# First modulation tile in two halves, third tile ahead of two weight quarters, two weight roundings ahead of the squares

## The reference

```
cond = silu(c)
mod = cond @ mod_w + mod_b                      # 1024 x 6144
shift1, scale1, gate1, shift2, scale2, gate2 = split(mod, 6)
h = rms_norm(x, norm1_g) * (1 + scale1) + shift1
proj = h @ w_in                                 # 1024 x 5832
q_m, k_m, v_m, o_m, i_m, f_m, c_q, c_kv, k_r, gate_pre = split(proj)
...                                             # mLSTM and latent attention, merged
x = x + gate1 * mixer
...                                             # mixture of experts, then the second block
```

## Time and profile before

| what | us |
|---|---|
| runs | 1007.26, 1012.1, 1012.5 (median 1012.1) |
| the profiled execution | 1009.17 |
| its span, first to last instruction | 1007.4 |
| PE, DVE, ACT, POOL busy | 961.9, 492.1, 385.9, 380.5 |

### The profile page before, as it was taken

How to read it: one execution, slowest core, us unless ns; L and a number is a source line. 1 busy time by engine, 2 the same in 40 slices (tenths; PEclk the granted TensorE clock), 3 DMA queues, 4 the chain that set the end, 5 groups by cost and what they waited for, 6 DMA issues and landing times.

```text
span 1007.4 us, 15224 instructions
## 1 busy us (share of the span) xinstructions
PE 961.9 (95%) x6116; PEld 705.8 (70%) x6116; DVE 492.1 (49%) x863; ACT 385.9 (38%) x617; POOL 380.5 (38%) x249
## 2 busy tenths in 40 slices
PE   8999999999999999888898999999999999999997
PEld 4876687777878444443343899777556789999996
DVE  2355177536144632321222513546766378777775
ACT  4343354445343321211121644544552353434342
POOL 3665666435773055353320689730003400000000
PEclk9999999999999999999999999999999999999999
DMA  9997964333769999999999788523224466353511
GB/s 371 403 382 305 356 196 122 105 109 101 250 215 422 377 419 416 408 412 411 412 411 370 282 317 263 146 84 112 98 74 139 164 272 236 140 229 146 220 72 42
DMA packets 50554, 252.08 MB, mean 250 GB/s; under 512 B 10688, under 2 KB 11328, under 8 KB 33728
## 3 DMA queue, kind: packets, MB, share of 16 engines
q1 hardware_dynamic: 44016, 248.10, 65.2%
q0 software_dynamic: 6480, 3.17, 1.1%
HBM read 294.22 MB, written 1.05 MB: 293 GB/s over the span
## 4 chain that ended last, share of the span: by engine, by line
PE 72%; DMA 11%; DVE 9%; ACT 3%; issue 2%; another core or an unknown queue 1%; SPq 0%; POOL 0%; DVEq 0%; POOLq 0%; ACTq 0%
PE ps L944 30%; PE ps L1269 17%; DMA big<-in_pieces_dram 5%; PE ps L1408 3%; DMA big<-in_mod_dram 3%; PE ps L1484 2%; PE ps L1435 2%; PE ps L1423 2%; PE ps L1365 2%; DMA cst<-in_pieces_dram 2%; PE ps L890 1%; PE ps L833 1%; DMA ring<-in_wa_dram 1%; PE ps L1173 1%
## 5 line engine op out<-in xcount | busy, mean ns | idle before, releaser
L2326 POOL TENSOR_TENSOR wl<-ring,wh 128x1024 fp32r<-128x1024 f32 (+5 forms) x128 | 279.2, 2200 | 228.2 <-ACT wh L1821 223.7
L1821 ACT ACTIVATE wh<-ring 128x1024 fp32r<-128x1024 f32 (+5 forms) x144 | 138.9, 979 | 131.6 <-PE ps L944 98.4
L944 PE MATMUL ps<-wh,hTh 128*128 128x512 f32 (+3 forms) x384 | 152.2, 396 | 3.3 <-DVE hTl L2516 2.0
L944 PE MATMUL ps<-wl,hTh 128*128 128x512 f32 (+3 forms) x384 | 147.3, 384 | 0.0
L944 PE MATMUL ps<-wh,hTl 128*128 128x512 f32 (+3 forms) x352 | 134.9, 383 | 0.0
L1269 PE MATMUL ps<-hTs,wsp 128*128 128x256 f32 x1056 | 128.9, 283 | 0.8 <-DVE wsp L3011 0.8
L1269 PEld LDWEIGHTS ps<-hTs,wsp 128*128 128x128 f32 x1056 | 128.1, 192 | 1.9 <-DVE wsp L3011 1.2
L2318 POOL TENSOR_TENSOR small<-small 128x2 f32<-128x2 f32 (+2 forms) x7 | 5.3, 760 | 263.1 <-DVE small L3324 192.8
L944 PEld LDWEIGHTS ps<-wh,hTh 128*128 128x128 f32 x384 | 72.1, 188 | 27.6 <-issue 8.9
L944 PEld LDWEIGHTS ps<-wl,hTh 128*128 128x128 f32 x384 | 72.3, 188 | 12.6
L944 PEld LDWEIGHTS ps<-wh,hTl 128*128 128x128 f32 x352 | 66.1, 188 | 12.9
(11 more groups left out here) (500 smaller groups left out, 1670.1 us busy)
## 6 DMA issues: line engine op xcount, KB each, us to landing
big<-in_pieces_dram SPq DMA_DIRECT2D x34, 2048.0 KB
ring<-in_wa_dram SPq DMA_DIRECT2D x64, 512.0 KB, 4.4
big<-in_mod_dram SPq DMA_DIRECT2D x12, 2048.0 KB, 11.6
ring<-in_ffn_dram SPq DMA_DIRECT2D x11, 2048.0 KB, 9.1
ring<-in_wb_dram SPq DMA_DIRECT2D x40, 512.0 KB, 3.6
dring<-in_ffn_dram SPq DMA_DIRECT2D x11, 1024.0 KB, 5.0
tenth<-in_pieces_dram SPq DMA_DIRECT2D x8, 1024.0 KB
ring<-in_wb_dram SPq DMA_DIRECT2D x12, 384.0 KB, 5.3
```

Source lines behind the costliest of these rows:

```text
L944: mm = pe.matmul(out, x[i], y[j], start=(p, c, k) == (0, 0, 0), stop=(c, k) == (KD - 1, 2), skip_group_check=True)
L1821: nc.scalar.activation(quarter(name, q, "high"), quarter(name, q, "raw"), ACT.Copy).then_inc(s_qh, 1)
L2326: nc.gpsimd.tensor_tensor(quarter(name, q, "low"), quarter(name, q, "raw"), quarter(name, q, "high"), ALU.subtract).then_inc(s_ql, 1)
```

## The change

SP loads the first tile as two halves of 1 MB, each with 128 columns of shift and of scale for one feature chunk, with the first weight quarter between them. Tile 1 stays behind quarter 0 of `ckr` and `qk0`; tile 2 is issued behind quarter 1 of `cq`, ahead of quarter 1 of `ckr` and of `qk0`. PE, ACT and DVE handle the first two chunks one by one, with a half each. The first row block's squares move from ACT to DVE. Ten of 38 fillers go. ACT rounds quarter 0 of `qk1` ahead of the copies of `ckv` and quarter 1 ahead of the latents' squares. The constants are counted on the semaphore of the vectors; counts of `s_gemv`, `s_mpart`, `s_msum` and `s_mev` shift by one.

```diff
@@ SP
+            def mod_half(h):
+
+                sp.dma_start(mhalf[:, h], mod[0].rearrange("p (h c n) -> p h c n", h=2, c=KD)[:, h]
+                             ).then_inc(s_half if h else s_mt[0], 16)
...
-            for q in range(2):
-                mod_tile(q)
-                for name in ("cq", "ckr", "qk0"):
-                    first_quarter(name, q)
+            mod_half(0)
+            first_quarter("cq", 0)
+            mod_half(1)
+            first_quarter("ckr", 0)
+            first_quarter("qk0", 0)
+            mod_tile(1)
+            first_quarter("cq", 1)
             mod_tile(2)
+            first_quarter("ckr", 1)
+            first_quarter("qk0", 1)
@@ PE
+            def half_rows(h):
+
+                pe.wait_ge(s_half if h else s_mt[0], 16)
+                for c in range(KD):
+                    q = c % 4
+                    mm = pe.matmul(ps[32 * q:32 * q + 32, 6, 256 * h:256 * h + 256], condw[:, c, 3:35], mhalf[:, h, c, :],
+                                   start=(c < 4), stop=(c >= 4), skip_group_check=True)
+                mm.then_inc(s_gemv, 1)
...
+            def half_sum(h):
+
+                pe.wait_ge(s_mpart, h + 1)
+                for i in range(2):
+                    at = 256 * h + P * i
+                    mm = pe.matmul(ps[:, 7, KD * i + h:KD * i + h + 1], mpart[:, 0, at:at + P], ones[:, 0:1],
+                                   start=True, stop=True)
+                mm.then_inc(s_msum, 1)
...
-            filler(38, 5)
+            filler(28, 5)
             pe.wait_ge(s_cond, 1)
-            mod_rows(0)
-            pe.wait_ge(s_const, 16)
+            half_rows(0)
+            pe.wait_ge(s_vec, 32)
             turn_rows(0)
-            mod_sum(0)
-            for b in range(1, 4):
-                turn_rows(b)
-            split_quarter(LI["cq"], 0)
+            half_sum(0)
+            turn_rows(1)
+            half_rows(1)
+            turn_rows(2)
+            half_sum(1)
+            first_quarter(0)
+            turn_rows(3)
+            first_quarter(1)
             mod_rows(1)
@@ ACT
-                for t in range(NT):
-                    link(nc.scalar.activation(hn[:, t, :], xs[:, t, :], ACT.Square,
-                                              accum_out=small[:, 16 + t:17 + t]))
-                act.nop().then_inc(s_ss, 1)
+                nc.scalar.activation(hn[:, 1, :], xs[:, 1, :], ACT.Square, accum_out=small[:, 17:18]).then_inc(s_ss, 1)
...
             weights_high(LI["cq"], (0,))
+            half_columns(0)
             weights_high(LI["ckr"], (0,))
-            first_columns(0)
+            half_columns(1)
             weights_high(LI["qk0"], (0,))
...
+            weights_high(LI["qk1"], (0,))
             grouped(act, "ckv")
             for t in range(NT):
                 ins = nc.scalar.copy(raw[:, t, 392:RAW], bank("ckv")[:, t * KVL:(t + 1) * KVL])
             ins.then_inc(s_ga, 1)
+            weights_high(LI["qk1"], (1,))
             act.wait_ge(s_ga, 3)
...
             act.nop().then_inc(s_ss, 1)
-            weights_high(LI["qk1"])
+            weights_high(LI["qk1"], (2, 3))
@@ DVE
+            dve.wait_ge(s_x, 16)
+            link(V.scalar_tensor_tensor(hn[:, 0, :], xs[:, 0, :], 1.0, xs[:, 0, :], ALU.mult, ALU.mult,
+                                        accum_out=small[:, 16:17]))
             norm_rows(0)
-            mod_part(0)
-            first_scales(0)
...
-            first_rest(0)
-            first_low(0)
-            for b in range(1, 4):
+            half_part(0)
+            half_scales(0)
+            half_low(0)
+            half_part(1)
+            keep_turned(1)
+            half_scales(1)
+            half_low(1)
+            for b in range(2, 4):
                 keep_turned(b)
```

More of the change, by code:

```diff
@@ L252, in build @@
         mtile = [part("mtile0", place["qnT"][0], KD, 512), part("mtile1", place["qnT"][0] + KD * 512, KD, 512)]
+        mhalf = part("mhalf", place["mtile0"][0], 2, KD * 256).rearrange("p h (c n) -> p h c n", c=KD)
         assert after("mtile1") <= after("ya")
@@ L447, in build @@
         ps = ctx.enter_context(nc.psum_tensor("ps", [P, 8, 512], F32))
-        s_vec, s_const, s_table, s_x, s_brow, s_final, s_out = (
-            sem(n) for n in ("s_vec", "s_const", "s_table", "s_x", "s_brow", "s_final", "s_out"))
+        s_vec, s_half, s_table, s_x, s_brow, s_final, s_out = (
+            sem(n) for n in ("s_vec", "s_half", "s_table", "s_x", "s_brow", "s_final", "s_out"))
         s_ring = [sem("s_ring0"), sem("s_ring1")]
@@ L653, in mod_tile, with load, load_into @@
                 if before:
-                    sp.wait_ge(s_gemv, before[-1] + 1)
+                    sp.wait_ge(s_gemv, before[-1] + 2)
                 sp.dma_start(mtile[n], mod[j].rearrange("p (c n) -> p c n", c=KD)).then_inc(s_mt[n], 16)
-            def load(name, stream):
+            def mod_half(h):
+                sp.dma_start(mhalf[:, h], mod[0].rearrange("p (h c n) -> p h c n", h=2, c=KD)[:, h]
+                             ).then_inc(s_half if h else s_mt[0], 16)
+            def load(name, stream, quarters=(0, 1, 2, 3)):
                 n = NL[name]
-                load_into(name, stream, n >= 2 and n - 2)
-            def load_into(name, stream, last):
+                load_into(name, stream, n >= 2 and n - 2, quarters)
+            def load_into(name, stream, last, quarters=(0, 1, 2, 3)):
                 n = NL[name]
@@ L669, in load_into @@
                     return
-                for q in range(4):
+                for q in quarters:
                     if last is not False and ALL[last][0] in LI:
@@ L827, in mod_rows @@
                 tiles = SUMS[SUM_OF[j]]
-                if i >= 1 and j == tiles[0]:
-                    pe.wait_ge(s_mpart, SUM_OF[j])
+                if j == tiles[0]:
+                    pe.wait_ge(s_mpart, SUM_OF[j] + 1)
                 at = 3 - tiles.index(j)
@@ L923, in outputs_of, with first_quarter @@
                         for n, a in enumerate(range(2 * P * j, min(2 * P * (j + 1), width), P))]
+            def first_quarter(c):
+                load, groups = SPLIT[0]
+                pe.wait_ge(s_ql, turn(0, 0) + 1)
+                if c == 0:
+                    pe.wait_ge(s_cond, 2)
+                else:
+                    pe.wait_ge(s_hTv, 1)
+                for name in groups:
+                    for out, operands in outputs_of(name):
+                        for k, (i, j) in enumerate(((0, 0), (0, 1), (1, 0))):
+                            x, y = operands(c)
+                            mm = pe.matmul(out, x[i], y[j], start=(c, k) == (0, 0), stop=False, skip_group_check=True)
+                if c:
+                    mm.then_inc(s_qu, 1)
             def split_quarter(n, q):
@@ L1795, in scaled_rows, with half_columns @@
                 nc.scalar.activation(hn[:, 1, :], xs[:, 1, :], ACT.Copy, scale=small[:, 19:20]).then_inc(s_hn[1], 1)
+            def half_columns(c):
+                act.wait_ge(s_mev, c + 1)
+                act.wait_ge(s_tr, 1)
+                nc.scalar.activation(hTh1[:, c, :], xT_column(c), ACT.Identity, scale=modT[:, 32 + c:33 + c],
+                                     bias=modT[:, c:c + 1]).then_inc(s_hTa if c else s_condt, 1)
             def first_columns(b):
-                act.wait_ge(s_mev, b + 1)
+                act.wait_ge(s_mev, b + 2)
                 act.wait_ge(s_tr, b + 1)
@@ L1909, in _ @@
             act.wait_ge(s_ctr, 1)
-            act.wait_ge(s_gemv, NMOD)
+            act.wait_ge(s_gemv, NMOD + 1)
             latent_high(0, 4)
@@ L2436, in mod_part @@
                 i = SUM_OF[j]
-                dve.wait_ge(s_gemv, SUMS[i][-1] + 1)
+                dve.wait_ge(s_gemv, SUMS[i][-1] + 2)
                 if i >= 2:
-                    dve.wait_ge(s_msum, i if j == 6 else i - 1)
+                    dve.wait_ge(s_msum, i + 1 if j == 6 else i)
                 V.tensor_copy(mpart[:, i % 2, :], ps[:, 6, :]).then_inc(s_mpart, 1)
@@ L2444, in gate_part @@
                 i = SUM_OF[j]
-                dve.wait_ge(s_gemv, j + 1)
-                dve.wait_ge(s_msum, i)
+                dve.wait_ge(s_gemv, j + 2)
+                dve.wait_ge(s_msum, i + 1)
                 link(V.tensor_copy(gate_hl[:, 0, :], ps[:, 6, :]))
@@ L2475, in norm_rows, with half_part, half_scales, half_low @@
                 V.tensor_scalar(hn[:, 0, :], xs[:, 0, :], small[:, 18:19], None, ALU.mult).then_inc(s_hn[0], 1)
+            def half_part(h):
+                dve.wait_ge(s_gemv, h + 1)
+                cs = slice(256 * h, 256 * h + 256)
+                V.tensor_copy(mpart[:, 0, cs], ps[:, 6, cs]).then_inc(s_mpart, 1)
+            def half_scales(c):
+                dve.wait_ge(s_msum, c + 1)
+                link(V.tensor_tensor(modT[:, c:KD + c + 1:KD], ps[:, 7, c:KD + c + 1:KD], v("mod1")[:, c:KD + c + 1:KD],
+                                     ALU.add))
```

(14 more changed lines are left out.)

18 lines of the change are left out of this document (9 added, 9 removed).

## The result

| | before | changed |
|---|---|---|
| median of 6 runs | 1011.45 us | 1020.23 us |
| lowest to highest | 1007.26 to 1015.52 | 1017.35 to 1023.05 |
| profiled execution, its span | 1009.17, 1007.4 | 1020.45, 1018.7 |
| mean granted clock of the span | 0.997 | 0.989 |

The ratio is 1.0088, with a 95% interval of 1.0066 to 1.0109: the change makes the kernel slower by some 9 us. The forecast was 1011.5, with 1005 to 1015; the time lies outside, on the side that had 0.08.

What follows compares the result with a forecast made beforehand. PE, busy 95%, bounds it, paced by queue landings; the early 1.4 gain becomes 0.6 late, the 1.41 becomes a DVE wait: 1009.17 + 0.6 = 1009.8 us profiled. Stated median 1011.5, range 1005 to 1015.

Steps and rivals of the forecast that it cites:

- the side that had 0.08: Whole kernel: chance given to a result slower by more than 0.5% (5 us), beside same 0.83 and faster 0.09.
- rival A: At `cq` 1: `ckr` 1 lands early, at 26.6, giving -1.0 there and at the end, 1008.2; chance 0.22.
- rival C: In the transfer queue: a fixed price per split transfer moves all by 2.0 us, +2.6 in total, 1011.8; chance 0.04.
- the gain is given back: From 58 to 89 us: PE's gain of 1.41 becomes a wait for DVE, so nothing of it survives.
- signs of being wrong: `ckr` 1 landed by 26.6, granted clock below 1.00 before 60 us, or PE's passage at 89 over 1.2 from 89.8.
- rival D: All parts gain: -1.7 at tile 2's rows and -1.4, neither ACT's order nor DVE's run binding, 1006.1; chance 0.09.
- The columns to the end of the low part: Ahead of `cq` 1: hidden columns 2 and 3 to their low part take 2.81 us, ending at 31.9.
- ACT's order: Ahead of `cq` 1: ACT waits for `ckr` 1 until 28.2 with the columns behind it, making PE 0.6 us later.
- the length of DVE's run ahead of the gate's sum: Run started by the conv's tanh, behind `v0` 0's rounding; its gate part ended at 71.36 before, PE wanting it at 71.57.
- 0.2 of slack: At the gate's sum, 71.57: PE is only 0.2 us behind DVE's run.
- the vanished 1.41: Ahead of `qk1`, near 60 us: early roundings remove PE's wait of 1.41 for `wl`.
- Rival B: Idle of about 2.2 us ahead of `cq` 1 lowers the clock, costing 1.7; +2.3 in total, 1011.5; chance 0.13.

Runs made afterwards that it cites:

- experiment 8: Changed kernel with ACT writing hidden columns 2 and 3 ahead of rounding `ckr` 1, and the first conv's tanh ahead of rounding `v0` 0; 1006.69 us, ratio 0.9962.
- experiment 3: Changed kernel with POOL waiting for DVE's hidden columns 2 and 3 before its low part of `ckr` 1; 1014.61 us, ratio 1.0061.
- experiment 5: Kernel before with only the queue order changed, tile 2 ahead of quarter 1 of `ckr` and `qk0`; 1018.67 us, ratio 1.0074.
- experiment 9: Changed kernel with 26 more matmuls on zeros ahead of `cq` 1, where PE idled; 1018.01 us, ratio 1.0057.
- experiment 2: Changed kernel with the four roundings of `qk1` behind the squares again, halves and queue order kept; 1019.29 us, ratio 1.0092.
- experiment 6: Kernel before with only the early roundings of `qk1`, ahead of the copies of `ckv` and of the squares; 1013.51 us, ratio 1.0030.
- experiment 7: Changed kernel with the old queue order and old roundings, leaving the halves, split squares and ten fewer fillers; 1010.46 us, ratio 0.9994.
- experiment 4: Changed kernel with ACT writing hidden columns 2 and 3 ahead of rounding quarter 1 of `ckr`; 1010.47 us, ratio 1.0008.

## Why the prediction was wrong

**What was right.** Half 0 landed 7.4 us after its issue, at 9.5 (9.1 forecast), half 1 at 13.0 (12.6). Tile 1's rows start at 20.20, behind a wait for its DMA (19.8 to 20.1). `ckr` 1 landed at 28.2, as taken:

```profile
big<-in_mod_dram SPq DMA_DIRECT2D x1, 1024.0 KB, 7.4
...
ring<-in_wa_dram SPq DMA_DIRECT2D x1, 384.0 KB, 13.7
```

(issued at 2.11 and 14.54). So rivals A and C are out: the landing wasn't early, and the split tile paid nothing near 2.0 us (`cq` 1 landed at 21.1 for 20.7). Tile 2's rows start at 28.10 (27.8), ACT's columns at 29.01 (29.1). The wait for `wl` is gone, and the gain is given back ahead of the gate's sum, as said. Two of the prediction's signs of being wrong came: a granted clock of 0.53 over 33 to 40 us, and the passage at `v1` at 98.5 in place of 89.8. What rival D priced, neither ACT's order nor DVE's run in the way, came only with two places of ACT's list changed as well (experiment 8, whose profiled execution took 1006.09; that D said 1006.1 is chance to this digit).

**The step that failed** is "The columns to the end of the low part took 28.76 + 0.69 - 26.64 = 2.81". The term was read from a stretch in which POOL was idle until DVE's last part began, in the kernel before:

```profile
27.84 0.88 DVE L2509 SCALAR_TENSOR_TENSOR hT<-hT,modT,hTh 128x256 f32<-128x256 f32 x2 [1.24 <-ACT hTh L1802]
...
28.76 2.94 POOL L2326 TENSOR_TENSOR third<-dring,wh 128x1024 fp32r<-128x1024 f32 x1 [2.17 <-ACT wh L1821]
```

(POOL even paid there: 2.94 for the 2.39 of this shape, beside DVE's 0.69.) I used it for a stretch in which POOL had just been handed three subtractions: by the same wait at `ckr` 1 that I had put into the sum, ACT rounds `ckr` 1 and starts POOL at 29.18, and DVE at 30.21. It measured 36.02 - 29.01 = 7.0. Of the +4.8 at `cq` 1, 0.4 to 0.6 is the landing and ACT's order (experiment 3 and the forecast) and the rest the hold. The order alone shows it too (experiment 5), and POOL held back takes it away with all else in place (experiment 3). So the hold at this place is shown, and not only argued.

**The second term of the same kind** is the length of DVE's run ahead of the gate's sum, which I took as fixed. In the changed kernel the rounding that starts it is at 71.49 for 65.26, 6.2 later, and DVE's gate part ends at 79.29 for 71.36, 7.9 later: the 1.7 between is the product's 2.48 for 0.75. PE, 4.9 late by `qk1`, with 0.2 of slack, waits 7.9 - 4.9 - 0.2 = 2.8 there; the trace has 2.73. So 1.7 of this wait is the hold, and the other 1.0 is what came back of the vanished 1.41, as forecast.

**Rival B** had the clock at the right place ahead of `cq` 1 and near the right price (1.7, measured 1.55), but behind an idle of 2.25 in place of 6.1, and without the second place, an idle of 2.7 with 1.53 behind it. Neither it nor the forecast had the hold. Together: 4.81 at `cq` 1, + 1.55 clock, - 1.47 for the wait for `wl`, + 2.88 at the gate's sum, + 1.53 clock = 9.30 at `v1`, against 8.9 by the ratio of the runs. That filling the idle gives the clock back is shown for the first place alone (experiment 9). By parts the ratios give +7.5 for the order, +3.0 for the roundings and -0.6 (none that can be told from zero) for the halves; the sum 9.9 stands beside 8.9 for all three. Each has an interval of 1.5 to 2.5 us to either side, and order with halves but without the roundings (experiment 2) gave 9.3, so the totals alone don't split the loss; the starts of PE do.

**What should have warned me** was in the trace before: a `CAST` of 128x2, the row at 67.75 shown above, took 2.15 us inside POOL's 16.98, where an instruction of that size takes 0.17. I read POOL's run as cover, since it was off the path. And the Trainium skill, page "SBUF — State Buffer", section "Who interferes with whom", says that a DVE instruction with two SBUF inputs and a GpSimd instruction that reads SBUF can't have the shared port at once: whichever starts first keeps it for its whole instruction and the other blocks. I didn't weigh it. The traces agree on both sides: 2.48 for 0.75 where POOL started first, 2.86 for 2.40 on POOL where DVE did, and no hold for `hn<-ps`, which has one input in PSUM. As an estimate made afterwards by that rule of the Trainium skill, with durations of the changed kernel's trace: POOL's three subtractions from 29.2 on end near 35.4 (1.83 + 2.39 + 2.02), the low part 0.5 behind the last, and `cq` 1 starts at 36, where it did.

**Still open:** why the clock is low behind 168 us in experiments 2 and 6. The profiled execution of the changed kernel is some 2 us later at the end (11.3) than at `v1` (9.3). Its lateness stays at 9.2 up to 310 us; it grows by 1.7 up to 345 us, where the granted clock is 0.74 and 0.83 (338 to 342, 342 to 346), moves between 8.4 and 11 up to 520 us, and grows by 1.2 near 768 us, where the clock is 0.57 (766 to 770). The kernel before has 1.00 at the same work both times. What lowers the clock there isn't shown. Of the twelve totals only those of experiments 6 and 7 lie inside what was expected; the others miss it by 0.4 to 2.3 us, while most of the starts and waits of PE up to `v1` came as expected. So an effect of one or two us on the total isn't resolved here.

## What to carry to other kernels

When a change moves an instruction of VectorE, or moves when GpSimd is handed its work, lay the two engines' timelines over each other at the new times, also where neither is the bound: a duration measured beside an idle neighbour isn't the duration beside a busy one. In these traces the hold hides inside the held instruction's own time: it shows as a longer busy time of a known shape and not as a wait of DVE; look for one shape with two durations. And when a queue's order is changed, change the order of the engine that consumes it in the same step (experiments 4 and 8), or the first late landing stands in front of work that was ready.

## What the runs showed of the hardware

- The hold works in both directions and is decided by who starts first: 0.1 us of lead made it 0.46 us on POOL, 0.5 us of lag made it 1.7 us on DVE.
- It took in an instruction with a single SBUF input: the `CAST` of 128x2 took 2.15, 2.12 and 2.10 beside POOL and 0.17 in its pause (experiment 8). The Trainium skill, page "SBUF — State Buffer", section "Who interferes with whom", names two SBUF inputs, or DVE's modes that use both port pairs, and has a cast among the operations that can enter them; whether this `CAST` did the traces don't show.
- An idle of about 2 us didn't decide the clock by its length: 2.0 for `hTl` in the kernel before and 2.03 in experiment 3 left it at 1.00, 1.95 in experiment 5 was followed by 0.66 over 19 to 24 us. Nor did 2.31 in experiment 4 lower it (1.00), where 2.73 in the changed kernel was followed by 0.57. Rival B's point of 2.2 us, from which I had it decide, doesn't hold.
